# Pooled rows read twice, and weight pieces waited for one by one, in an mLSTM mixer's output projection

## The reference, cut to what matters

```python
proj = jnp.einsum('bsd,dp->bsp', h, w_in)            # q, k, v, o, gates, u
hm = h_fwd + h_bwd                                    # two scans over 8 chunks of 128 positions, 4 heads
hm = hm * lax.rsqrt(jnp.mean(hm * hm, axis=-1, keepdims=True) + EPS)   # by head
y_a = jax.nn.sigmoid(o) * hm * g_head                 # 512 columns
y_b = _multiscale_pool(u, w_pool, pool_scale)         # 512 columns, from u alone
y = jnp.concatenate([y_a, y_b], axis=-1)
x = x + gt1 * jnp.einsum('bsm,md->bsd', y, w_out)     # 1024 x 1024 by 1024 x 1024
```

## Time and profile before

| | |
|---|---|
| times of three runs | 2693.12, 2699.9, 2702.52 us; median 2699.9 |
| profiled execution | 2699.14 us; from first to last instruction (the span) 2697.3 |
| mean granted clock of PE | 0.972 |
| busy: PE, DVE, ACT, POOL | 2501.9, 1596.1, 1208.2, 842.3 us |
| the stretch of w_out's 16 groups | 1944.4 to 2034.5 us of the span |

### The profile page before, as it was taken

The page is one execution under the profiler, slowest core; times in us unless marked ns, Lnnn a source line. Parts: engine busy times, 40 slices in busy tenths (PEclk is TensorE's granted clock), DMA queues, the critical chain, the costliest instruction groups (busy, mean ns, idle before and its releaser), DMA issues.

```text
span 2697.3 us, 32759 instructions
## 1 busy us (share of the span) xinstructions
PE 2501.9 (93%) x11852; PEld 2034.1 (75%) x11852; DVE 1596.1 (59%) x2803; ACT 1208.2 (45%) x2228; POOL 842.3 (31%) x740
## 2 busy tenths in 40 slices
PE   4997899999999899999999999998598999999997
PEld 3765778886778677777888886887586888878886
DVE  5347459988463786875545853246647444355676
ACT  6146347745312644454334443235326555543343
POOL 0222432221210355553242400004003656514242
PEclk9998999999999899999999998999798999999999
DMA  4102123324252267768854432222332444396444
GB/s 157 46 16 77 44 65 92 102 98 142 78 195 101 81 202 228 218 215 265 277 175 149 156 106 74 83 78 73 107 134 77 157 155 147 125 343 198 133 157 155
DMA packets 190131, 369.82 MB, mean 137 GB/s; under 512 B 13692, under 2 KB 58372, under 8 KB 189716
## 3 DMA queue, kind: packets, MB, share of 16 engines
q1 hardware_dynamic: 177620, 340.46, 38.5%
q0 software_dynamic: 4288, 12.60, 1.4%
q10 hardware_dynamic: 8064, 14.68, 1.4%
HBM read 266.95 MB, written 100.74 MB: 136 GB/s over the span
## 4 chain that ended last, share of the span: by engine, by line
PE 75%; DVE 11%; DMA 5%; ACT 4%; issue 3%; POOL 1%; SPq 0%; DVEq 0%; ACTq 0%; POOLq 0%
PE bank L2651 7%; PE bank L2653 7%; PE bank L2652 7%; PE bank L2269 7%; PE bank L2270 7%; PE bank L2271 7%; PE bank L2624 5%; PE bank L2625 5%; PE bank L2626 5%; PE bank L2446 3%; PE bank L2448 3%; PE bank L2447 3%; DMA ada<-in_w_ada 3%; DVE ada_sum L1918 2%; PE bank L2366 1%
## 5 line engine op out<-in xcount | busy, mean ns | idle before, releaser
L2624 PE MATMUL bank<-hq_hi,wq_hi 128*128 128x512 f32 x896 | 356.2, 398 | 17.6 <-DVE hq_lo L1926 12.1
L2651 PE MATMUL bank<-ring_b_hi,ring_a_hi 128*128 128x512 f32 x896 | 350.3, 391 | 5.5 <-DVE hidden L1906 5.1
L2625 PE MATMUL bank<-hq_lo,wq_hi 128*128 128x512 f32 x896 | 353.5, 395 | 0.0
L2626 PE MATMUL bank<-hq_hi,wq_lo 128*128 128x512 f32 x896 | 353.4, 394 | 0.0
L2653 PE MATMUL bank<-ring_b_hi,ring_a_lo 128*128 128x512 f32 x896 | 349.9, 391 | 0.0
L2652 PE MATMUL bank<-ring_b_lo,ring_a_hi 128*128 128x512 f32 x896 | 349.6, 390 | 0.0
L2018 DVE TENSOR_TENSOR ring_a_lo<-a_raw,ring_a_hi 128x1024 fp32r<-128x1024 f32 x112 | 152.2, 1359 | 224.5 <-ACT ring_a_hi L1292 224.3
L1292 ACT ACTIVATE ring_a_hi<-a_raw 128x1024 fp32r<-128x1024 f32 x112 | 118.7, 1060 | 328.7 <-PE bank L2653 307.6
L2624 PEld LDWEIGHTS bank<-hq_hi,wq_hi 128*128 128x128 f32 x896 | 171.0, 191 | 57.8 <-DVE hq_lo L1926 17.8
L1865 DVE TENSOR_TENSOR wq_lo<-unit_raw,wq_hi 128x512 fp32r<-128x512 f32 x160 | 158.0, 993 | 87.7 <-ACT wq_hi L1158 85.5
L2651 PEld LDWEIGHTS bank<-ring_b_hi,ring_a_hi 128*128 128x128 f32 x896 | 168.7, 188 | 41.3 <-DVE hidden L1906 5.9
(11 more groups left out here) (450 smaller groups left out, 5576.0 us busy)
## 6 DMA issues: line engine op xcount, KB each, us to landing
a_raw<-hidden_scratch SPq DMA_DIRECT2D x112, 512.0 KB, 3.3
hidden_scratch<-hidden SPq DMA_DIRECT2D x32, 1024.0 KB, 5.1
w_raw<-in_w_in SPq DMA_DIRECT2D x104, 256.0 KB, 2.8
ada<-in_w_ada SPq DMA_DIRECT2D x96, 256.0 KB, 3.0
hidden_scratch<-hidden SPq DMA_DIRECT2D x32, 768.0 KB, 4.5
unit_raw<-in_w_mlp_in SPq DMA_DIRECT2D x16, 1024.0 KB, 8.4
b_raw<-in_w_mlp_out SPq DMA_DIRECT2D x32, 512.0 KB, 4.6
unit_raw<-in_w_ff SPq DMA_DIRECT2D x16, 1024.0 KB, 5.4
```

What stands on the lines that cost most here:

```text
L2624: mm(o, lh[:, q, :], rh[:, q, :], start=(fresh and q == 0), stop=False, skip_group_check=True)
L2625: mm(o, lh[:, q, :], rl[:, q, :], start=False, stop=False, skip_group_check=True)
L2626: l = mm(o, ll[:, q, :], rh[:, q, :], start=False, stop=(q == 3), skip_group_check=True)
L2651: mm(o, ra_hi[r][:, e, js], rb_hi[r][:, e, :], start=(fresh and v == 0 and e == 0), stop=False, skip_group_check=True)
```

## The change

Three edits in the second mixer.

The first: SP loads the pooled rows of the first 512 positions a second time, hi and lo (2 MB in all), into `ybe`, the first half of W[0], after the first four `row_spread` loads. PE multiplies them with chunk 21's pieces 4 to 7 right after the recurrence's last products, into banks 0 to 3 (4 tiles of 12 matmuls, banks left open). When the values of half 0 are ready it adds pieces 0 to 3 (another 12 each) and only then increments `group_done`. The pooled rows are still loaded into yT[0] for chunk 22, now last in the queue; the residual rows of half 0 are loaded behind sg load 1 in place of 3. Because `ybe` lies in W[0], the hi parts of chunk 22 wait until the first four groups are done (`group_done` at GO2+4).

The second: DVE scales only half 0 of hsum first, makes value n+1 ahead of low part n, and scales half 1 between the low parts 2 and 3.

The third: in `transposed` (chunks 17 and 20) the first group waits piece by piece in place of `chunk_ready`.

```diff
+        ybe = [at(f"yb_early_{n}", [P, 4, HALF], f32r, 8192 * i) for i, n in enumerate(("hi", "lo"))]
...
+            def pooled_rows(h, o):
+
+                for x, d in zip(o, (yh_d, yl_d)):
+                    sp.dma_start(x.bitcast(f32), d[:, h * HALF:(h + 1) * HALF].rearrange("(k p) q -> p k q", p=P))\
+                        .then_inc(yb_in[h], 16)
+
             for m in range(4):
                 spread(m)
+            sp.wait_ge(p_out, 16 * 16)
+            pooled_rows(0, [x[:, :, :] for x in ybe])
             load_chunk(C_OUT2 + 1, kpieces(a["w_out_2"][0], 512, 512), range(NRAW))
             for m in range(4, 16):
                 spread(m)
             sp.wait_ge(m_h, 16)
-            sp.wait_ge(p_out, 16 * 16)
...
-                if n in (3, 7):
-                    h = n // 4
-                    sp.wait_ge(y_tr, 4 * h + 4)
-                    for o, d in zip(yT[h], (yh_d, yl_d)):
-                        sp.dma_start(o[:, 4:8, :].bitcast(f32), d[:, h * HALF:(h + 1) * HALF]
-                                     .rearrange("(k p) q -> p k q", p=P)).then_inc(yb_in[h], 16)
+                if n == 7:
+                    sp.wait_ge(y_tr, 8)
+                    pooled_rows(1, [o[:, 4:8, :] for o in yT[1]])
+                if n in (1, 7):
                     sp.dma_start(xs[:, 4 * h:4 * h + 4, :], x1_d[:, 4 * h:4 * h + 4, :]).then_inc(x2_in[h], 16)
+            pooled_rows(0, [o[:, 4:8, :] for o in yT[0]])
             load_chunk(C_OUT2 + 1, kpieces(a["w_out_2"][0], 512, 512), range(NRAW, 8))
...
-            split_hi(C_OUT2 + 1, 0, GO2)
+            split_hi(C_OUT2 + 1, 0, GO2 + 4)
...
+            head_scaled(0)
+            y_value(0)
+            for n in range(8):
+                if n == 3:
+                    head_scaled(1)
+                if n < 7:
+                    y_value(n + 1)
+                y_low(n)
...
+            def pieces_ready(c):
+
+                return lambda k: pe.wait_ge(w_lo, 8 * c + k + 1)
...
             def transposed(c, g0, behind=lambda n: None):
...
-                chunk_ready(c)
...
-                                                (h2[h][0][:, k, :], h2[h][1][:, k, :])) for k in range(8)])
+                                                (h2[h][0][:, k, :], h2[h][1][:, k, :])) for k in range(8)], need=None if n else pieces_ready(c))
...
+            W2 = W[C_OUT2 % 2]
+
+            def half_product(t, pairs, first):
+
+                for k, ((lh, ll), (rh, rl)) in enumerate(pairs):
+                    mm(bank[t][:, :], lh, rh, start=(first and k == 0), stop=False)
+                    mm(bank[t][:, :], lh, rl, start=False, stop=False)
+                    l = mm(bank[t][:, :], ll, rh, start=False, stop=(not first and k == 3))
+                return l
+
+            chunk_ready(C_OUT2)
+            pe.wait_ge(yb_in[0], 32)
+            for t in range(4):
+                q = slice(t * P, (t + 1) * P)
+                if t == 2:
+                    pe.wait_ge(m_nx, 16)
+                half_product(t, [((ybe[0][:, k, q], ybe[1][:, k, q]), (W2[0][:, 4 + k, :], W2[1][:, 4 + k, :])) for k in range(4)],
+                             True)
             for n in range(8):
                 pe.wait_ge(y_n, 8 * (n // 4 + 1))
...
-            y_half(0)
-            by_token(C_OUT2, GO2, 512, yT, lambda: y_half(1))
+            pe.wait_ge(y_lo, 4)
+            for t in range(4):
+                half_product(t, [(tok(yT, k, t), (W2[0][:, k, :], W2[1][:, k, :])) for k in range(4)], False).then_inc(group_done, 1)
+            pe.wait_ge(y_lo, 8)
+            for t in range(4, 8):
+                group(GO2 + t, t % 4, 512, [(tok(yT, k, t), (W2[0][:, k, :], W2[1][:, k, :])) for k in range(8)],
+                      need=(lambda k: pe.wait_ge(yb_in[1], 32) if k == 4 else None) if t == 4 else None)
+            pe.wait_ge(yb_in[0], 64)
             by_token(C_OUT2 + 1, GO2 + 8, 512, yT)
```

More of the change, by code:

```diff
@@ L2216, in _, with head_scaled, y_value @@
             link(tt(q_, q_, r_, ALU.mult))
[L2217 to L2220, removed]
+            def head_scaled(h):
+                for t in range(4 * h, 4 * h + 4):
+                    x = hsum[h][:, t % 4, :].rearrange("p (h e) -> p h e", h=4)
+                    tt(x, x, hss[:, 0, 4 * t:4 * t + 4].unsqueeze(2).broadcast_to([P, 4, P]), ALU.mult).then_inc(y_n, 2)
+            def y_value(n):
                 dve.wait_ge(y_tr, n + 1)
@@ L2226, in _, with y_low @@
                     ALU.mult, ALU.mult).then_inc(y_v2, 1)
+            def y_low(n):
                 dve.wait_ge(y_hi, n + 1)
@@ L2263, in _, with product @@
             mm = nc.tensor.matmul
-            def product(out, pairs):
+            def product(out, pairs, need=None):
                 n = len(pairs)
                 for i, ((lh, ll), (rh, rl)) in enumerate(pairs):
+                    if need:
+                        need(i)
                     mm(out, lh, rh, start=(i == 0), stop=False)
@@ L2272, in product, with group @@
                 return last
-            def group(g, b, width, pairs, rows=P):
+            def group(g, b, width, pairs, rows=P, need=None):
                 if not (isinstance(g, int) and g < 4):
                     pe.wait_ge(group_free, g - 3)
-                product(bank[b][0:rows, 0:width], pairs).then_inc(group_done, 1)
+                product(bank[b][0:rows, 0:width], pairs, need).then_inc(group_done, 1)
+            def pieces_ready(c):
+                return lambda k: pe.wait_ge(w_lo, 8 * c + k + 1)
             def chunk_ready(c):
@@ L2821, in _ @@
                 l.then_inc(y_tr, 1)
-            def y_half(h):
-                pe.wait_ge(y_lo, 4 * h + 4)
-                pe.wait_ge(yb_in[h], 32)
-            y_half(0)
-            by_token(C_OUT2, GO2, 512, yT, lambda: y_half(1))
+            pe.wait_ge(y_lo, 4)
[6 more added lines that the diff above has]
+            pe.wait_ge(yb_in[0], 64)
             by_token(C_OUT2 + 1, GO2 + 8, 512, yT)
```

## The result

The changed kernel took 2683.39 us (median of 5 runs, 2673.23 to 2690.8) against 2699.9 (2693.12 to 2702.52): a ratio of 0.9934, with a 95% interval of 0.9907 to 0.9962. The profiled execution has a span of 2681.6 us, 15.7 less than before.

What follows compares the result with a forecast made beforehand. A 24.4 us gap with 32 PE transposes, then a block bound by PE alone, bound this stage. Gains of 3.5 + 0 + 10.9 + 1.5 = 15.9 us gave 2684, likeliest case 2680 to 2689, overall range 2678 to 2692.

Steps and rivals of the forecast that it cites:

- Chunk 17: PE before chunk 17: starting piece by piece removes the wait for the last lo piece, gaining 3.5 us.
- Second copy: SP's queue after spread 3: 2.1 MB more delays spread 4 within its 8.6 us slack; cost 0, bound 2 us.
- Half products: PE's gap after the recurrence: 48 matmuls run at clock 1.00 in 10.9 us, done at 1930.9.
- The rival at 0.50: Half products run at the slow clock, about 21 us; all behind 10 us later, 6 gained, 2694; chance 0.07.
- Where the groups resume: End of the gap: groups resume at 1944.4 as before, transposes ending last; bounds 1 us earlier to 3 later.
- The block and its clock: Block after the gap: 48 of 384 matmuls already done, 10.9 us less; fewer slow matmuls, 1.5 us more.
- Chunk 22: Chunk 22's hi parts, now behind the first four groups: 1.8 us of slack before a bank is wanted, cost 0.
- The slower rival: DVE held in chunk 22 by pieces 4 to 7 behind three 2.1 MB loads; 2707 if landing at 1993; chance 0.04.
- The sum: Whole kernel: 3.5 + 0 + 10.9 + 1.5 = 15.9 us less, giving 2684.0 beside the median.
- more than forecast: Slow stretch behind chunk 17's first group stays away: up to 6.6 us more gained, 2677; chance 0.07.

Runs made afterwards that it cites:

- e1: Kernel before with only the third edit (first group of chunks 17 and 20 waits piece by piece): 2693.56 us, ratio 0.9993.
- e5: The changed kernel itself, unaltered, run once more on one chip beside a version with another DVE order: 2683.27 us, ratio 0.9934 to the kernel before.
- e9: Changed kernel with the pooled rows of the first half loaded once more, into an unread place, ahead of the second copy: 2684.2 us, ratio 0.9946.
- e2: Changed kernel without the third edit, the piece by piece wait: 2685.76 us, ratio 0.9957.
- e7: Changed kernel with four slots for sg in place of two, DVE's order unchanged: 2682.88 us, ratio 0.9931.
- e10: Changed kernel with four sg slots, scaling of half 1 on ACT, and low part 3 ahead of value 4: 2673.2 us, ratio 0.9899.
- e3: Changed kernel with DVE's old order, all eight tiles scaled first, then value n and low part n in turn: 2675.86 us, ratio 0.9929.
- e4: Changed kernel with half 1 scaled ahead of value 2, and low part 3 ahead of value 4: 2676.96 us, ratio 0.9927.
- e6: Changed kernel with half 1 scaled in DVE's wait for sg load 2 and low part 3 ahead of value 4, run again: 2678.89 us, ratio 0.9926.

## Why the prediction was right

**Chunk 17: right.** Forecast 3.5 us; the wait of 3.52 is gone, and A is 3.8 (after) and 3.9 (e1) shorter at the same slow time in it (20.4 to 20.6 us at 0.50). The slow stretch moved along. That it was equally long in these executions is luck: in e5, the changed kernel again, it was not (see the last section).

**Second copy: the cost was right, with less to spare than taken.** The forecast took 0 with a bound of 2, out of 8.6 us of slack, of which the transfer was to use 5.4 to 8.7. B is unchanged (73.74 against 73.76), but some 6.5 us of the slack went and only 2.0 were left. What was mis-sized is SP's own issue, put at some 1 us, for which no row was given: the two loads held SP for 1.49 and 2.59 us, and with the loads behind them spread 4 was issued 9.8 us after the first spread against 6.4 before; it then took 9.8 us to land in place of 6.7. e9 shows the step behind this edge.

**Half products: right.** 48 in 11.0 us at 1.00. The rival at 0.50 did not come. The Trainium skill, TensorE: Matmul & The Clock Gate, section Part 1: The HAM clock gate, calls the throttled state the default, which activity releases. By that rule products behind a thin stretch begin slow; in e2, e7, e9 and e10 they did, but for a few matmuls only (12 us for all 48, 1 us lost), never the 10 us of that rival, and in the other six with half products all 48 took 11 us.

**Where the groups resume: right, to 0.3 us.** Shifted by the 3.5 us of chunk 17 the forecast is 1940.9; the first group's row begins at 1941.16. The parts agree: half products done at 1927.4 (forecast 1927.4), value 0 at 1927.97 (1928.0), second transposes last. sg load 2 took 3.7 us to land, not 3.1, and the residual rows were in at about 1931.2, ahead of it. (PE itself does not wait for the residual rows: before, they landed at 1949.3, 5 us behind PE's first product with w_out. DVE does, at the first bank that it empties of either half.) So the change pays here with one wait for another: the DMA wait of 3.3 us for the pooled rows is gone, and V is still 1.6 us longer. e3, e4 and e7 show why: the second edit puts value 2 before sg load 2 has landed, and the scaling behind it. With the old order or the scaling in that wait V is 8.2 to 8.4, and from the first half product to the groups it is 21.4 or 20 us in place of 24.8. The prediction took the second edit as given and did not weigh it against the old order, so it got the start right and missed that this edit costs 3.4 us, as e3 shows.

**The block and its clock: right.** Forecast 10.9 + 1.5 = 12.4 us less in D; measured 90.11 - 77.62 = 12.5.

**Chunk 22: right.** No bank was waited for. Bank 1 was empty at 1956.85 and its next group began at 1958.74: 1.9 us of slack, 1.8 forecast. Pieces 4 to 7 of chunk 22 reach ACT at 1961.21, behind the 6.3 MB of rows:

```profile
1953.56 2.20 ACT L936 ACTIVATE w_hi<-w_raw 128x512 fp32r<-128x512 f32 x4 [8.02 <-PE bank L2849]
1961.21 2.61 ACT L936 ACTIVATE w_hi<-w_raw 128x512 fp32r<-128x512 f32 x4 [5.46 <-DMA w_raw<-in_w_out]
```

```profile
1941.61 0.43 SPq L654 DMA_DIRECT2D yT_hi<-yb_hi_scratch  x1
...
1943.96 0.56 SPq L654 DMA_DIRECT2D yT_lo<-yb_lo_scratch  x1
...
yT_lo<-yb_lo_scratch SPq DMA_DIRECT2D x1, 1024.0 KB, 16.5
```

The slower rival had these rows in at 1960.6, or 1957.1 when shifted by the 3.5 us of chunk 17. The last landed at 1960.5: 18.9 us from the first issue in place of 16, 333 GB/s in place of 390. So its transfer was put too fast, but not by enough to matter: bank 3, emptied behind the lo parts of the first two of these pieces, was empty at 1964.6, and its next group began at 1969.6.

**The sum.** 3.8 - 0.3 + 12.5 = 16.0 in A, C and D, 15.9 forecast; the span fell by 15.7. The rival "more than forecast" gave the slow stretch behind chunk 17 a chance to stay away. It stayed in every execution, but came shorter in some, by chance and not by an edit (below); in e5, the same program, that gave 3.2 us more.

What stays open: what decides between the two lengths of B, 72.5 and 73.7 us, which no edit touches. Most of the difference is the masked spread of the third to the tenth step, 0.68 us in the one and 0.79 in the other, and it goes with the place of a POOL operation beside it (vw, the weighted values). Two rows of after, then two of e4:

```profile
1860.63 0.79 DVE L2166 TENSOR_TENSOR Ew<-row_spread,dmask 128x512 f32<-128x512 f32 x1
1861.10 0.80 POOL L910 TENSOR_SCALAR vw<-vx,ecols 128x129 f32<-128x129 f32 x1
```

```profile
1863.15 0.68 DVE L2166 TENSOR_TENSOR Ew<-row_spread,dmask 128x512 f32<-128x512 f32 x1
1863.21 1.09 POOL L910 TENSOR_SCALAR vw<-vx,ecols 128x129 f32<-128x129 f32 x1
```

Where POOL starts 0.46 to 0.47 us behind DVE, DVE takes 0.78 to 0.79; where it starts 0.06 to 0.26 behind, DVE takes 0.68 and POOL 0.89 to 1.10 in place of 0.80. That holds for these eight steps in all executions but e9, where two steps fall outside. after and e5 both have the long form, e4 and e6 both the short one; why POOL falls in the one place or the other is not shown.

## What to carry to other kernels

When work is pulled into a gap, the gap's length belongs to the chain that runs through it: here the pulled work was free at either place, and what was left to win (5 us from the half products to the groups, 6 in e10) lay in the order of one engine's queue around one late DMA. A load put ahead of others in one queue costs them its transfer and also the issuer's time, so count the slack of the next load by both. When such a load comes late, PE can pay twice, in the wait and in products at 0.50 behind it (e9). Where executions of one program differ by more than an edit is worth, compare stages between two events of the same execution.

## What the runs showed of the hardware that was not expected

SP's issue of a 1 MB load of pooled rows took 0.43 to 0.74 us at the block's start (four of them, the last with some 5 MB ahead of it), and 1.49 and 2.59 right behind the first four spreads, with 1 MB and 2 MB ahead.

Within A PE is slow in two places, behind chunk 17's first group and, in most executions, some 60 us later. Ahead of both it has small products to do: 16 matmuls on 16 rows (L2744, L2745) in the first place, 40 on 8 rows (L2752, L2755) in the second. Two windows of the changed kernel and then the same two of e5, the same program, each at the same distance from A's start:

```profile
1627.60:1660.00 32.40, 32.40 (x101) 18.98 (x100) 11.72 (x17) 10.29 (x17) 0.00 (x0) 0.79 0.31 95
1680.00:1700.00 20.00, 20.00 (x100) 16.72 (x99) 7.90 (x17) 6.52 (x11) 0.00 (x0) 0.83 0.60 187
```

```profile
1631.10:1663.50 32.40, 32.40 (x108) 19.41 (x108) 11.88 (x17) 10.44 (x17) 0.00 (x0) 0.84 0.32 101
1683.50:1703.50 20.00, 20.00 (x107) 16.68 (x107) 6.61 (x12) 6.37 (x11) 0.00 (x0) 0.91 0.60 182
```

Twice the window's length times (1 - clock) is the time at 0.50: 13.6 + 6.8 = 20.4 us in the one, 10.4 + 3.6 = 14.0 in the other, and half the difference, 3.2 us, is the difference in A. Added up so over all of A, in windows of 5 us, it is 20.4 to 20.6 us in before, after and e1, 23.9 in e2, 10.2 in e6, and 13.6 to 13.7 in all others. A less half of that is 197.2 to 198.2 us in every kernel with the third edit, and 201.2 (before) and 199.9 (e2) without it. So nearly all of the scatter of A is clock, and beside it the third edit is worth 3.9 us (before against e1) or 2.5 (e2 against after). The Trainium skill, TensorE: Matmul & The Clock Gate, section Part 1: The HAM clock gate, calls the number of slow matmuls at a kernel's start variable from run to run of one kernel. Here the same is seen of a stretch inside a kernel: 20.5 us in after and 13.7 in e5.

The same code ahead of chunk 17 is reached at 1624.5 us in one execution and at 1634.3 in another, and at 1627.6 and 1631.1 in after and e5, one program. With A, this may be most of the scatter of some 10 us within the times of one kernel, and it is why e5 and e6 needed their stages; it is not shown, since one execution of each run was profiled.
